# A hybrid decoder layer on one core: order of the input stage, and who normalises every third tile

## The reference, cut to what matters

```python
def layer_norm(x, g, b):
    mu = jnp.mean(xf, axis=-1, keepdims=True)
    var = jnp.mean(jnp.square(xf - mu), axis=-1, keepdims=True)
    return ((xf - mu) * lax.rsqrt(var + EPS) * g + b)
...
xp = layer_norm(x_prompt, ln_in_g, ln_in_b)
xs = layer_norm(x_sample, ln_in_g, ln_in_b)
...
p = jnp.einsum('btd,dp->btp', h, w_in) + b_in
```

## Time and profile before

| what | us |
|---|---|
| median of 3 runs | 1256.51 |
| lowest, highest | 1248.21, 1258.26 |
| profiled execution, its time | 1249.1 |
| its span, first to last instruction | 1247.3 |

### The profile page before, as it was taken

The page is one execution under the profiler, slowest core; times in us unless marked ns, Lnnn a source line. Parts: engine busy times, 40 slices in busy tenths (PEclk is TensorE's granted clock), DMA queues, the critical chain, the costliest instruction groups (busy, mean ns, idle before and its releaser), DMA issues.

```text
span 1247.3 us, 22260 instructions
## 1 busy us (share of the span) xinstructions
PE 1127.9 (90%) x8055; PEld 669.3 (54%) x8055; DVE 722.9 (58%) x1685; ACT 419.9 (34%) x989; POOL 185.3 (15%) x247
## 2 busy tenths in 40 slices
PE   6999999999999999888888889999649999999970
PEld 4676776866866455666566655445333333333320
DVE  6935665856745012468889863346764444334886
ACT  4322523425323010348788853213200111011431
POOL 0122031310311000220110100000010111112233
PEclk8999999999999999979999999999759999999995
DMA  9841030130201403221720026300476979586994
GB/s 297 268 133 34 22 83 1 41 64 20 85 1 53 123 4 65 89 82 25 195 80 19 2 79 180 119 34 18 173 268 229 353 247 302 187 292 232 353 333 151
DMA packets 127752, 166.41 MB, mean 133 GB/s; under 512 B 32305, under 2 KB 101249, under 8 KB 127654
## 3 DMA queue, kind: packets, MB, share of 16 engines
q1 hardware_dynamic: 112502, 111.48, 29.7%
q0 software_dynamic: 15152, 53.60, 11.8%
HBM read 227.92 MB, written 36.47 MB: 212 GB/s over the span
## 4 chain that ended last, share of the span: by engine, by line
PE 77%; DVE 12%; DMA 3%; issue 3%; ACT 2%; SPq 1%; POOL 1%; DVEq 0%; POOLq 0%; ACTq 0%
PE act L742 19%; PE vec L1375 11%; PE vec L777 8%; PE vec L1101 8%; PE vec L752 5%; PE vec L1008 3%; PE act L1388 2%; PE vec L1388 2%; PE act L1023 2%; PE vec L793 2%; DVE arena L2123 2%; PE act L1035 2%; DVE arena L2139 1%; DMA arena<-x_rows,arena 1%; PE act L1048 1%
## 5 line engine op out<-in xcount | busy, mean ns | idle before, releaser
L742 PE MATMUL act<-arena 128*128 128x352 f32 x768 | 237.0, 464 | 0.0
L742 PEld LDWEIGHTS act<-arena 128*128 128x128 f32 x768 | 143.4, 190 | 76.4 <-issue 1.2
L1375 PE MATMUL vec<-arena 128*64 128x512 f32 x768 | 174.3, 606 | 2.0 <-DMA arena<-in_exp_w 2.0
L1101 PE MATMUL vec<-arena 128*128 128x512 f32 x256 | 112.9, 594 | 0.8 <-DVE arena L2148 0.8
L1375 PEld LDWEIGHTS vec<-arena 128*64 128x64 f32 x768 | 53.8, 139 | 103.0 <-issue 101.3
L777 PE MATMUL vec<-arena 128*128 128x512 f32 (+1 forms) x256 | 100.3, 546 | 0.0
L1627 ACT ACTIVATE arena<-arena 128x640 f32<-128x640 f32 (+15 forms) x128 | 82.6, 660 | 8.9 <-DVE arena L2123 8.2
L1617 ACT COPY arena<-act 128x64 f32<-128x64 f32 (+7 forms) x256 | 70.9, 361 | 41.9 <-PE act L1023 41.8
L2473 DVE TENSOR_SCALAR arena<-arena 128x256 f32<-128x256 f32 x24 | 7.3, 306 | 131.7 <-ACT arena L1724 131.7
L1101 PEld LDWEIGHTS vec<-arena 128*128 128x128 f32 x256 | 47.4, 189 | 58.2 <-issue 56.8
L2123 DVE CUSTOM_DVE_ANT_0 arena<-vec,arena 128x128 f32<-128x128 f32 (+7 forms) x144 | 63.7, 465 | 14.9 <-PE act L1023 3.7
(11 more groups left out here) (468 smaller groups left out, 1878.8 us busy)
## 6 DMA issues: line engine op xcount, KB each, us to landing
arena<-in_exp_w SPq DMA_DIRECT2D x192, 512.0 KB
arena<-in_exp_w SPq DMA_DIRECT2D x48, 1024.0 KB
y_rows<-arena POOLq DMA_DIRECT2D x24, 512.0 KB, 5.9
arena<-in_w_in SPq DMA_DIRECT2D x16, 512.0 KB, 6.8
arena<-in_x_prompt SPq DMA_DIRECT2D x8, 512.0 KB, 5.7
x_spill<-arena POOLq DMA_DIRECT2D x8, 512.0 KB, 3.4
arena<-x_spill SPq DMA_DIRECT2D x8, 512.0 KB, 4.9
arena<-in_cache_fox_kv SPq DMA_DIRECT2D x16, 256.0 KB, 3.5
```

Of the source, the lines that this page charges most:

```text
L742: last = mm(bk[:, 0:n], W[k % 2][:, c, m * P:(m + 1) * P], xT[:, c, a:a + n], start=c == 0, stop=c == NC - 1)
L1101: last = mm(bk[:r], src, Wo[half][:, c, :], start=c == 0, stop=c == NC - 1)
L1375: last = mm(gu_bank[p][o], xgT[p][:, c, o], Wgu[:, slot, c, :], start=c == 0, stop=c == NC - 1)
```

## The change

- SP issues weight block 1 between the sixth and the seventh tile of x. The other three blocks stay where they were.
- PE does piece 0 right after group 0's turns, with a wait for each chunk of `xT` ahead of that chunk's product in place of one for all, then group 1's turns, group 2's turns, and pieces 1 to 8.
- ACT copies out piece 0 between group 0's and group 1's chunks. The square roots stay ahead of chunk 6.
- POOL normalises the last tile of each group (tiles 2, 5 and 8); DVE the first two.
- DVE scales only tile 0 ahead of group 2's even chunks, and tiles 1 to 8 after them.

```diff
--- before.py
+++ after.py
@@ -509,7 +509,10 @@
         E = Engine(ev, e, "sync")
         xp, xs = I["x_prompt"][0], I["x_sample"].rearrange("b t d -> (b t) d")
         e.dma_start(onehot[0:33, :], I["bucket_rows"]).then_inc(*E.moved("bucket_in"))
+        first_at, first_from, _ = w_blocks[0][1]
         for t in range(NT):
+            if t == 6:
+                e.dma_start(W[0][:, :, first_at:first_at + P], w_view[:, :, first_from:first_from + P]).then_inc(*E.moved("first1_in", ("w_in", 0, 1)))
             e.dma_start(X1[:rows(t), t, :], xp[t * P:(t + 1) * P] if t < 8 else xs).then_inc(*E.moved(f"x{t}_in"))
             if t == 2:
                 e.dma_start(ident, I["consts"][:, 0:P]).then_inc(*E.moved("ident_in"))
@@ -524,7 +527,7 @@
             if k >= 2:
                 e.wait_ge(*E.at(("w_in used", k - 2)))
             dst = W_nkvg if k == 6 else W[k % 2]
-            for a, c, n in ([w_blocks[0][x] for x in (1, 0, 2, 3)] if k == 0 else w_blocks[k]):
+            for a, c, n in ([w_blocks[0][x] for x in (0, 2, 3)] if k == 0 else w_blocks[k]):
                 e.dma_start(dst[:, :, a:a + n], w_view[:, :, c:c + n]).then_inc(*(E.moved(f"w{k % 2}_in", ("w_in", k)) if k else E.moved(f"first{a // P}_in", ("w_in", 0, a // P))))
 
         load_w(0)
@@ -739,6 +742,8 @@
             e.wait_ge(*E.free("act"))
             bk = E.bank("act")
             for c in range(NC):
+                if (k, m, third) == pieces_of(0)[0]:
+                    e.wait_ge(*E.at(("xT ready", 0, c)))
                 last = mm(bk[:, 0:n], W[k % 2][:, c, m * P:(m + 1) * P], xT[:, c, a:a + n], start=c == 0, stop=c == NC - 1)
             last.then_inc(*E.filled("act", ("w_in used", k)))
 
@@ -821,15 +826,15 @@
             bk = E.bank("act")
             e.transpose(bk[:, 0:P], ke_samples, ident).then_inc(*E.filled("act"))
 
-        for g in range(2):
-            turn_normal(g)
+        turn_normal(0)
         for n, piece in enumerate(pieces_of(0)):
-            if n < 3:
+            if n in (1, 2):
                 e.wait_ge(*E.at(("xT ready", n)))
             if n == 2:
                 e.wait_ge(*E.at("xT by vec"))
             project(*piece)
             if n == 0:
+                turn_normal(1)
                 turn_normal(2)
         e.wait_ge(*E.at(("w_in", 0, 3)))
         e.wait_ge(*E.at("consts_in"))
@@ -1435,7 +1440,7 @@
                 if ring in rings:
                     e.wait_ge(*E.full(ring))
                     bk = E.job(ring)
-                    act(xT[:, c, a:a + n], bk[:, 0:n], ACT.Identity, bias=lncol[:, 1, c:c + 1], scale=lncol[:, 0, c:c + 1]).then_inc(*E.drained(ring, ("xT ready", g)))
+                    act(xT[:, c, a:a + n], bk[:, 0:n], ACT.Identity, bias=lncol[:, 1, c:c + 1], scale=lncol[:, 0, c:c + 1]).then_inc(*E.drained(ring, ("xT ready", g), ("xT ready", g, c)))
 
         def transposed(dst, tag, tiles=range(NT)):
             for t in tiles:
@@ -1455,7 +1460,6 @@
             act(strip_tmp[0:H, a:a + n], bk[0:H, 0:n], ACT.Identity, scale=-1.0).then_inc(*E.drained("act", "strip rows"))
         e.wait_ge(*E.at("lncol_in"))
         turned(0)
-        turned(1)
         e.wait_ge(*E.at("bcol_in"))
         E.stage("hgrn")
 
@@ -1487,6 +1491,7 @@
         for n, piece in enumerate(pieces_of(0)):
             projected(*piece)
             if n == 0:
+                turned(1)
                 turned(2, ("act",))
             if n == 2:
                 softplus(0)
@@ -1803,22 +1808,22 @@
             r = rstd[:, tiles[0]:tiles[-1] + 1]
             ts(r, mv[:, tiles[0]:tiles[-1] + 1, 1], EPS, None, ALU.add).then_inc(*E.done(("variances", "ln0", g)))
             e.wait_ge(*E.at(("rstd", "ln0", g)))
-            e.reciprocal(r, r).then_inc(*E.done())
-            e.wait_ge(*E.own())
-            for t in tiles:
+            e.reciprocal(r, r).then_inc(*E.done(("rstd known", g)))
+            e.wait_ge(*E.own())
+            for t in tiles[:-1]:
                 x, r = X1[:rows(t), t, :], rows(t)
                 ts(x, x, mv[:r, t, 0:1], rstd[:r, t:t + 1], ALU.subtract, ALU.mult).then_inc(*E.done(("x normal", t)))
         e.wait_ge(*E.at("ln_in"))
 
-        def gain_and_shift(g):
+        def gain_and_shift(g, tiles):
             e.wait_ge(*E.at(("x transposed pe", g)))
-            for t in GROUPS[g]:
+            for t in tiles:
                 x, r = X1[:rows(t), t, :], rows(t)
                 tt(x, x, ln_g[:r], ALU.mult).then_inc(*E.done())
                 e.wait_ge(*E.own())
                 tt(x, x, ln_b[:r], ALU.add).then_inc(*E.done(("x scaled", t)))
 
-        gain_and_shift(0)
+        gain_and_shift(0, GROUPS[0][:1])
         a, n = GROUPS[2][0] * P, sum(rows(t) for t in GROUPS[2])
         E.jobs["vec"] = 7
         e.wait_ge(*E.at("lncol_in"))
@@ -1826,8 +1831,9 @@
             e.wait_ge(*E.full("vec"))
             bk = E.job("vec")
             ts(xT[:, c, a:a + n], bk[:, 0:n], lncol[:, 0, c:c + 1], lncol[:, 1, c:c + 1], ALU.mult, ALU.add).then_inc(*E.drained("vec", "xT by vec"))
-        gain_and_shift(1)
-        gain_and_shift(2)
+        gain_and_shift(0, GROUPS[0][1:])
+        gain_and_shift(1, GROUPS[1])
+        gain_and_shift(2, GROUPS[2])
         E.stage("p2")
         e.wait_ge(*E.at("hgrn_in"))
         e.wait_ge(*E.at("bcol_in"))
@@ -2583,6 +2589,12 @@
         tt = e.tensor_tensor
         e.dma_start(tab33[0:32, :], I["rel_bias_table"]).then_inc(*E.moved("tab_in"))
         e.dma_start(tab33[32:33, :], I["masked_row"]).then_inc(*E.moved("tab_in"))
+        E.stage("ln0")
+        for g, tiles in enumerate(GROUPS):
+            t = tiles[-1]
+            x, r = X1[:rows(t), t, :], rows(t)
+            e.wait_ge(*E.at(("rstd known", g)))
+            e.tensor_scalar(x, x, mv[:r, t, 0:1], rstd[:r, t:t + 1], ALU.subtract, ALU.mult).then_inc(*E.done(("x normal", t)))
         for t in range(NT):
             e.wait_ge(*E.at(("x scaled", t)))
             e.dma_start(x_spill[:rows(t), t * D:(t + 1) * D], X1[:rows(t), t, :]).then_inc(*E.moved("x_spill"))
```

## The result

The changed kernel takes 1259.24 us (median of 12 runs, 1256.23 to 1265.21), the kernel before 1250.83 (12 runs in the same comparison, 1247.14 to 1258.26). The ratio is 1.0055 with a 95% interval of [1.0035, 1.0075]: slower by 6.9 us, between 4.4 and 9.4. The two medians lie 8.4 us apart; the text goes by the ratio throughout. The profiled execution has a span of 1262.6 us.

The account below looks back on a forecast made before the run. PE bounds the kernel; its 3.15 us hole and low clock offered about 6 us. Turns of group 2 ending at 34.3 plus 2.0 for the clock gave +0.7, added to 1252.8: 1253.5 us, range 1246 to 1260.

Parts of the forecast that it names:

- the sum: End of group 2's turns: 34.3 plus 2.0 for the clock gives 36.3, 0.7 us later than 35.63.
- The nearest are its copy, 1.14 us, and its two-source product, 2.44.: GpSimd's normalisation of one tile: taken as 1.14 us, with 2.44 kept for the range.
- PE is busy with strips until 13.52, so it costs nothing.: Group 0's normalisation, ending at 13.1, hides behind PE's strip matmuls; at the upper bound it costs 1 us.
- The clock, 2.0 with an upper bound of 4.6.: Lower PE clock behind the new hole: 1.7 us in group 2's turns, 0.3 in the next piece; bounds 0 and 4.6.
- D: Rival: first weights land too late for piece 0 at 17.85, making everything behind it later; +3.1 us, chance 0.08.
- B: Rival: PE's clock stays full over the new hole ahead of group 2's turns; -1.3 us, or -2.4, chance 0.22.
- limit: No PE hole at all in the input stage: group 2's turns end at 29.5, -6.1 us.
- C: Rival: GpSimd's operation of 2.44 us holds up group 2's normalisation and the low clock takes 4.6; +4.5 us, chance 0.2.
- Row and rule agree: Shared ports: a vector operation waits for GpSimd's whole instruction, so normalisation times add, 2.64 us in place of 2.25.

Follow-up runs that it names:

- e4: Kernel before plus extra normalisations on spare columns, on GpSimd and the vector engine, where both idle, to price GpSimd's operation; a single execution, no time compared.
- r1: The changed kernel run once more, unaltered: +6.6 us [4.1, 9.1] against the kernel before.
- e10: e1 with 36 transposes of the identity added on PE in its hole: -1.9 us [-4.1, 0.5] against the kernel before.
- e9: e8 with piece 2 also waiting by chunk and the vector engine copying group 2's even chunks before any gain and shift: 1246.35 us, ratio 0.9941.
- e7: As e3, with the square roots for groups 1 and 2 ahead of chunks 4 and 2: +1.0 us [-1.4, 3.5] against the kernel before.
- e8: e1 with piece 1, waiting by chunk, between group 1's and group 2's turns: -5.1 us [-7.5, -2.9] against the kernel before.
- e6: Kernel before with only the first block of weights issued between the sixth and seventh tile of x: -1.1 us [-3.6, 1.4].
- e2: Kernel before with only the third tile of each group normalised by GpSimd: +3.3 us [0.6, 5.9].
- e3: e1 with the square root for group 2 ahead of chunk 3 instead of 6: -0.4 us [-3.5, 2.8] against the kernel before.
- r2: Changed kernel with 52 transposes of the identity on PE ahead of group 2's turns, second run: +4.6 us [2.4, 6.9] against the kernel before.
- e1: Changed kernel with the vector engine normalising all nine tiles, GpSimd none: +5.0 us [1.9, 8.1] against the kernel before.

## Why the prediction was wrong

It forecast next to no difference (+0.7 us at the end of group 2's turns and in the time); measured is +6.9, and the interval begins at +4.4. That the median of 1259.24 still lies inside the range of 1246 to 1260 is owed to the width that the scatter of the runs gave it, not to the sum. Half of the mechanism was right: a new hole ahead of group 2's turns, with the root behind piece 0 as one part of it, and a lower clock behind the hole. The other half was wrong: GpSimd's tile was to hide in group 0 and to add 0.39 us in group 2, and it is what PE waits for all three times. Three terms of the sum were too small, by its own steps:

- **"The nearest are its copy, 1.14 us, and its two-source product, 2.44."** The operation takes 4.32 (3.78 alone, e4). It lies above both bounds. I had bounded by the number of tensors read, and that doesn't carry over: even with a constant and one operation it takes 2.79, against 1.14 for the copy. The two columns and the second operation together add 1.0 to that, the rest of the distance to the copy is unexplained. This is the step that failed. On the path it cost 1.75 us at group 2 (4.39 from start to end instead of 2.64).
- **"PE is busy with strips until 13.52, so it costs nothing."** With 4.32 it costs PE 2.00 us of waiting; this follows from the first step. Turns start at 15.69, piece 0 ends 2.4 us later than forecast, the root at 29.28 instead of 26.7, 2.6 later. My upper bound here was 1. Some 0.6 us of it are this execution's own: the normalisation began at 11.04 instead of 10.45. In r1 it began at 10.47 and the wait was 1.65.
- **The clock, 2.0 with an upper bound of 4.6.** It cost 2.5 in the turns and 2.67 in the pieces, 5.2. The turns' 2.5 is the whole of the old price and not two thirds of it, and I let the low level end soon behind the turns as it had before; here it lasted 13.7 us in place of 6.8. What makes it last longer stays open.

Forecast end of the pieces 36.3 + 38.06 = 74.4; with 2.6, 1.75 and 3.2 added, 81.9, measured 82.04. So the loss is accounted for in this execution's stage; the repeat ended at 80.94, so that the sum closes to 0.1 us is luck.

Point by point for the rest. The weights landed in time (issued at 9.66, 7.2 us to landing by the profile, 16.9): D is out. Piece 0 ran at the full clock behind group 0's turns, not held by the waits by chunk. Group 1's tile was hidden but for 0.36. A shift passes on whole: shown up to 520 us, in all runs. B's upside was real but needed more than a kept clock: e10 gives -0.98 at the pieces (I had -1.3), e9 -5.05 of the "limit" of -6.1. I wrote that the limit needs the root ahead of group 1's copies; it didn't, piece 1 in the hole does it. The us that is missing lies in group 0's turns, which were over at 18.88 instead of 17.85. C was the rival that happened, with a price of 4.32 where I had 2.44; I gave it 0.2 because I took the copy's price as the nearest.

"Row and rule agree", on the shared ports, doesn't hold here: e4's third and fourth vector operations ran at 0.81 inside one GpSimd instruction, and in the changed kernel a two-source operation took 1.21 beside GpSimd's (32.01), against 1.23 where GpSimd is idle. What the vector engine lost was 0.8 us once per GpSimd operation (2.34 for two tiles instead of 1.5). The Trainium skill (SBUF — State Buffer, "SBUF: two separate sides") has the pair of ports locked for the whole instruction and the other engine fully blocked. For this GpSimd operation the measurement decides against that; for the two-source product of the earlier trace rows it stands.

The Trainium skill (GPSIMD Engine Reference, "Engine selection") calls one-input operations "roughly line-rate". This one isn't: 3.78 us for 1024 elements, against 1.14 for the copy.

The number itself, 1253.5, also leaned on reading four times as two values; twelve runs of the kernel before spread evenly from 1247 to 1258.

## What to carry to other kernels

When the trace lacks an operation on GpSimd, don't take its price from another kind of operation: the nearest row by tensors read was too low by almost a factor of four, and the one meant as the upper bound by 1.8. Measure it, as e4 does, or keep the upper bound open. When a step moves ahead on the bound engine, follow the small step that stands behind it on another engine (here a square root of three columns) to the next place where the bound engine waits. And fill a hole with work that is there, by chunk, rather than shorten it: e9, without a wait, kept the clock in the profiled execution, while it fell behind e7's hole of 2.3 us and e8's of 1.8. Look, too, at what stands right behind the limit that is lifted, as the old order's third piece does in e6.

## What the runs showed of the hardware

- The granted clock's lower level lasted 3.4 us in e4, e6 and e8, 6.8 in the kernel before, e2, e3, e7 and r2, and 13.7 in the changed kernel, r1 and e1, with PE busy without a break behind the hole in all of them. The length of the hole doesn't order them: behind 4.7 us (e2) it was 6.8, behind 4.25 (e1) 13.7. What decides isn't settled.
- It can fall after PE is busy again: in e8 1.1 us after PE had resumed from a wait of 1.8, in e3 2.1 us after a wait of 2.85. And a wait needn't lose it: the 2.00 us at 13.7 in the changed kernel left it at 1.00.
- The granted clock doesn't show every slow stretch: at 1.00 throughout, group 0's first chunks take 0.64 us each and the rest 0.33, and in r1, e2, e6 and e9 all eight take 0.64.
- GpSimd's two-operation normalisation costs the same for 32 rows as for 128, 4.31 and 4.32 us.
